# Two transformer blocks on one core: the convolution's sums kept in PSUM, the projections' low parts on GpSimd, layers written out, stage ends made ahead

## What is computed

```python
# first block, per layer
u = modulate(h, ...); y = swiglu_ffn(u, w_gate, w_up, w_down)          # d_ff 2816
h = layer_norm(ALPHA * h + 0.5 * gate * y)
y = hybrid_token_mixer(modulate(h, ...))                               # below
h = layer_norm(ALPHA * h + gate * y)
h = layer_norm(ALPHA * h + 0.5 * gate * swiglu_ffn(modulate(h, ...)))
# hybrid_token_mixer: one projection w_in, then three branches
y_a = silu(layer_norm(causal_dwconv(val * sigmoid(gate), width 31))) @ w_a_out
y_b = mamba2_ssd(...)  (a causal convolution of width 4 first)  @ w_b_out
y_c = nsa_attention(...) @ w_c_out
y = (g0 * y_a + g1 * y_b + g2 * y_c) @ w_o
# second block, per layer
z = rmsnorm(x) @ w_in; att = sliding_window_attention; hm = mlstm_chunkwise
x = x + (gates * (att @ w_att) + gates * (hm @ w_m)) @ w_out
x = x + relu(rmsnorm(x) @ w_ff1) ** 2 @ w_ff2                          # d_ff 4096
```

## Time and profile before

| | us |
|---|---|
| median of 3 runs | 3005.77 (2996.24 to 3027.09) |
| profiled execution, its own time | 3011.23 |
| its span | 3009.4 |
| mean granted TensorE clock in it | 0.944 |

### The profile page before, as it was taken

How to read it: one execution, slowest core, us unless ns; L and a number is a source line. 1 busy time by engine, 2 the same in 40 slices (tenths; PEclk the granted TensorE clock), 3 DMA queues, 4 the chain that set the end, 5 groups by cost and what they waited for, 6 DMA issues and landing times.

```text
span 3009.4 us, 53898 instructions
## 1 busy us (share of the span) xinstructions
PE 2719.9 (90%) x19972; PEld 2530.0 (84%) x19976; DVE 1863.7 (62%) x2968; ACT 1184.6 (39%) x1984; POOL 630.3 (21%) x386
## 2 busy tenths in 40 slices
PE   4998996799989979989788999997978999988999
PEld 4997996678789979979687878996976898876899
DVE  6755987656366675669884653774084575175476
ACT  2444442325334444434332552443442344342344
POOL 2322000000023323310000000332640244540243
PEclk9999997889999999999898999998988999997999
DMA  7757541222367377575322224763431455341453
GB/s 305 279 189 269 201 164 52 100 71 92 120 219 255 135 264 247 189 282 176 119 85 77 99 92 155 262 224 134 139 121 63 148 187 176 120 140 56 140 187 127
DMA packets 131947, 486.18 MB, mean 162 GB/s; under 512 B 15024, under 2 KB 15024, under 8 KB 130352
## 3 DMA queue, kind: packets, MB, share of 16 engines
q1 hardware_dynamic: 106704, 389.09, 37.1%
q0 software_dynamic: 23040, 83.90, 7.6%
q10 hardware_dynamic: 2016, 10.66, 0.9%
HBM read 478.34 MB, written 5.24 MB: 161 GB/s over the span
## 4 chain that ended last, share of the span: by engine, by line
PE 81%; DVE 10%; DVEq 2%; issue 2%; ACT 2%; DMA 2%; ACTq 0%; SPq 0%; POOL 0%; POOLq 0%
PE ps L429 19%; PE ps L431 18%; PE ps L430 18%; PE ps L680 5%; PE ps L2080 2%; PE ps L958 2%; PE ps L2090 2%; DVE ac L1516 2%; PE ps L535 1%; PE ps L440 1%; PE ps L439 1%; PE ps L438 1%; DMA qr<-ada_dram 1%; PE ps L481 1%; PE ps L898 1%
## 5 line engine op out<-in xcount | busy, mean ns | idle before, releaser
L430 PE MATMUL ps<-u_parts,high 128*128 128x256 f32 x3712 | 1060.7, 286 | 0.0
L430 PEld LDWEIGHTS ps<-u_parts,high 128*128 128x128 f32 x3712 | 716.4, 193 | 2.3
L1002 ACT ACTIVATE high<-ring 128x1024 fp32r<-128x1024 f32 x434 | 456.7, 1056 | 456.3 <-PE ps L431 338.4
L429 PE MATMUL ps<-ac_parts,high 128*128 128x256 f32 x1920 | 548.3, 286 | 27.2 <-DVE u_parts L1376 18.2
L429 PE MATMUL ps<-h_parts,high 128*128 128x256 f32 (+1 forms) x1792 | 524.9, 293 | 39.5 <-DVE u_parts L1376 14.8
L431 PE MATMUL ps<-ac_parts,ring_parts 128*128 128x256 f32 x1920 | 546.5, 285 | 0.0
L431 PE MATMUL ps<-h_parts,ring_parts 128*128 128x256 f32 (+1 forms) x1792 | 516.0, 288 | 0.0
L429 PEld LDWEIGHTS ps<-h_parts,high 128*128 128x128 f32 (+1 forms) x1792 | 347.8, 194 | 56.0 <-issue 20.1
L429 PEld LDWEIGHTS ps<-ac_parts,high 128*128 128x128 f32 x1920 | 368.5, 192 | 31.3 <-DVE u_parts L1376 13.3
L431 PEld LDWEIGHTS ps<-ac_parts,ring_parts 128*128 128x128 f32 x1920 | 366.6, 191 | 0.0
L429 PE MATMUL ps<-pt_parts,high 128*128 128x256 f32 x1216 | 345.1, 284 | 11.8 <-DVE pt_parts L1420 11.8
(11 more groups left out here) (391 smaller groups left out, 4500.3 us busy)
## 6 DMA issues: line engine op xcount, KB each, us to landing
ring<-stream_dram SPq DMA_DIRECT2D x736, 512.0 KB, 3.3
xc<-ada_dram POOLq DMA_DIRECT2D x80, 512.0 KB, 6.3
z<-ada_dram POOLq DMA_DIRECT2D x40, 512.0 KB, 8.4
qr<-ada_dram POOLq DMA_DIRECT2D x40, 512.0 KB, 11.2
h_aside<-h ACTq DMA_DIRECT2D x4, 1024.0 KB, 8.1
h<-h_aside ACTq DMA_DIRECT2D x4, 1024.0 KB, 6.3
par<-par_dram ACTq DMA_DIRECT2D x3, 365.0 KB, 6.5
conb<-con_dram ACTq DMA_DIRECT2D x1, 1088.0 KB, 8.7
```

The costliest lines, as they stand in the source:

```text
L429: mm(out, hi, xh, start=start, stop=False, **kw)
L430: mm(out, hi, xl, start=False, stop=False, **kw)
L1002: act(high_of(m, i), chunk_of(m, i), ACT.Copy).then_inc(sem["hi"], 1)
```

## The change

1. Wide and narrow convolution: the running sums are in PSUM banks 0 to 3 instead of SBUF; the last tap writes `ac` or `xc`. Channel tiles go in fours. No low part stands between the taps.
2. Low parts of the 69 chunks ahead of the branches: GpSimd, in order, with 8 loads of each of two modulation groups among them. The 16 gate chunks stay on VectorE.
3. `modulation_rows` after C_GLU pairs 1 and 4 and C_XBC pair 0. The mean of the wide convolution 8 chunks earlier (after C_Q pair 3), the mean of squares before C_VS.
4. Layers written out (Python loops); one continuous ring of slots over layers and blocks.
5. Stage ends: first high parts at the end of the stage before; first low parts among the residual; centred `h` goes to `ac` before the mixer, from where it is stored and read; `whole_h` after the first `hidden_low`; `u` and its low parts interleaved in the second block; parameters and `conb` of the second block loaded early; its first squares straight from the end of the first block; residual and output of the second block by pairs of tiles.
6. Last attention groups: the product with `w_c_out` is begun with six of eight tiles (`three_groups`) before the last values are there.

```diff
 class Stream:
+    def slot(self, l, i):
+        return (self.first(l) + i) % RING
@@ tensor1
         def low_made(i):
-            t.wait_ge(sem["lo_m"], at("lo_m", mix1(i) + 1))
+            if i < C_CK:
+                t.wait_ge(sem["lo_g"], at("lo_g", NF + mix1(i) + 1))
+            else:
+                t.wait_ge(sem["lo_m"], at("lo_m", mix1(i) - FRONT + 1))
...
-        accumulate_ones(0, m.ac, "aconv", 0, con("mean")).then_inc(sem["mu"], 1)
+            if n == 3:
+                t.wait_ge(sem["aconv"], at("aconv", 4))
+                accumulate_ones(0, m.ac, "aconv", 0, con("mean")).then_inc(sem["mu"], 1)
+        rms(1, m.sq_a, 1)
@@ scalar1
-            a.wait_ge(done, done_at(cb + 65))
+            for i in range(cb + 66, cb + 66 + HIGH):
+                later_high(i)
...
-        first_highs(C_MIX)
-        squares(0, m.h, m.u, "cent", 0, 5, park=True)
-        a.wait_ge(sem["aside"], at("aside", 16))
+        squares(0, m.ac, m.u, "cent", 0, 5, park=True)
         high_u(1, m.uhi)
@@ vector1
             low(cb + 3, HIGHS * q + 4)
-            whole_h(2 * q)
             hidden(0, 0)
             hidden_low(0, 0)
             low(cb + 5, HIGHS * q + 6)
+            whole_h(2 * q)
...
-        def conv(dst, src, w, b, taps, lo, hi, signal, between=(), lows=()):
+        def conv(dst, src, w, b, taps, lo, bank_, signal, between=()):
+            sums = lambda n: ps[:, bank_ + (n - lo) // 2, (n - lo) % 2 * S:(n - lo) % 2 * S + S]
             for k in range(taps):
-                for n in range(lo, hi):
+                for n in range(lo, lo + 4):
                     if k == 0:
-                        ts(dst[:, n], src[:, n, 0:S], par(w, n * taps), par(b, n), ALU.mult, ALU.add)
+                        ts(sums(n), src[:, n, 0:S], par(w, n * taps), par(b, n), ALU.mult, ALU.add)
+                    elif k < taps - 1:
+                        stt(sums(n), src[:, n, k:k + S], par(w, n * taps + k), sums(n), ALU.mult, ALU.add)
                     else:
-                        last = stt(dst[:, n], src[:, n, k:k + S], par(w, n * taps + k), dst[:, n], ALU.mult, ALU.add)
+                        stt(dst[:, n], src[:, n, k:k + S], par(w, n * taps + k), sums(n), ALU.mult, ALU.add)\
+                            .then_inc(sem[signal], 1)
-                if k < len(lows):
-                    low_mix(lows[k])
                 v.drain()
-        half = C_GLU + 11 + TAPS_A
-        conv(m.ac, m.apad, "aw", "ab", TAPS_A, 0, 4, "aconv", between=(3, 5, 7, 9), lows=range(C_GLU + 11, half))
-        conv(m.ac, m.apad, "aw", "ab", TAPS_A, 4, ND, "aconv", lows=range(half, C_VS))
+        conv(m.ac, m.apad, "aw", "ab", TAPS_A, 0, 0, "aconv", between=(3, 5, 7, 9))
+        keep_mixed()
+        conv(m.ac, m.apad, "aw", "ab", TAPS_A, 4, 2, "aconv")
@@ gpsimd1
+        for n, i in enumerate(range(C_MIX, C_CK)):
+            low(i)
+            for it, after in ((1, 6), (2, 13)):
+                if after <= n < after + 4:
+                    for k in range(2 * (n - after), 2 * (n - after) + 2):
+                        load_later(ada.group(l, 1, it), k)
@@ every engine, both blocks
-    with v.Fori(0, DEPTH) as l:
+    for l in range(DEPTH):
         layer(l)
@@ scalar2
-        a.wait_ge(sem["layer_done"], at("layer_done", 1))
-        a.dma_start(m.par[:, 0:PAR2["all"]], par_source[bass.ds(l, 1)].rearrange("a p n -> (a p) n"))\
-            .then_inc(sem["par"], 16)
-        a.dma_start(aside, m.h).then_inc(sem["aside"], 16)
@@ vector2
             for n in range(ND):
-                last = stt(m.u[:, n], m.h[:, n], par(gain, n), m.rs, ALU.mult, ALU.mult)
-                last.then_inc(sem["umod"], 1)
+                stt(m.u[:, n], m.h[:, n], par(gain, n), m.rs, ALU.mult, ALU.mult).then_inc(sem["umod"], 1)
+                if n >= 1:
+                    low_u(k, n - 1, uhi)
+            low_u(k, ND - 1, uhi)
```

More of the change, by code:

```diff
@@ L902, in values, with three_groups, last_group @@
             last.then_inc(sem["pv"], 1)
+        def three_groups(n):
+            i = C_PC + n
+            t.wait_ge(landed[stream.slot(l, i)], landed_at(i))
+            for k in range(6):
+                mm(ps[:, 4 + n, 0:S], chunk_tile(m, i, k), m.oT[:, k], start=k == 0, stop=False)
+        def last_group(n):
+            i = C_PC + n
+            for k in range(6, ND):
+                last = mm(ps[:, 4 + n, 0:S], chunk_tile(m, i, k), m.oT[:, k], start=False, stop=k == ND - 1)
+            last.then_inc(done, 1)
         def gate_product(n, bank):
@@ L1382, in whole_h, with residual @@
                     .then_inc(sem["whole"], 1)
-        def residual(k0, i, place, ready):
+        def residual(k0, i, place, ready, lows):
             v.wait_ge(sem["based"], at("based", i + 1))
@@ L1547, in layer @@
             last.then_inc(sem["kpe"], 1)
+        inverse_root(1)
+        for n in range(ND):
+            tt(m.ac[:, n], m.ac[:, n], m.rs, ALU.mult).then_inc(sem["anrs"], 1)
         j = 31
@@ L1920, in pair @@
             return j + 1
-        j = pair(E_Q, j)
+        t.wait_ge(sem["lo_g"], at("lo_g", E_Q + 2))
+        for k in range(ND):
+            t.wait_ge(sem["ulo"], at("ulo", k + 1))
+            for c in range(2):
+                last = product3(mm, ps[:, unit(3 * c), c * S:(c + 1) * S], m, E_Q + c, k, m.uhi2[:, k], m.ulo[:, k],
+                                start=k == 0, stop=k == ND - 1, skip_group_check=True)
+                if k == ND - 1:
+                    last.then_inc(done, 1)
+        j += 1
         j = pair(E_Q + 2, j)
@@ L2115, in down @@
                              m.hidlo[:, f % 3], start=False, stop=last, skip_group_check=True)
+                if last and n in (1, 3, 5):
+                    x.then_inc(pairs, 1)
             x.then_inc(done, 1)
-        up(E_FFN, 0, 0)
+        t.wait_ge(sem["lo"], at("lo", 1))
+        for k in range(ND):
+            t.wait_ge(sem["ulo"], at("ulo", 8 + k + 1))
+            last = product3(mm, ps[:, 4, 0:S], m, E_FFN, k, m.uhi_ffn[:, k], m.ulo[:, k],
+                            start=k == 0, stop=k == ND - 1)
+        last.then_inc(done, 1)
         with t.Fori(0, 3) as it:
@@ L2126, in layer, with scalar2 @@
         down(E_FFN + 63, 31, 31, last=True)
-    with t.Fori(0, DEPTH) as l:
+    for l in range(DEPTH):
         layer(l)
-def scalar2(nc, a, m, sem, stream, par_source, aside):
+def scalar2(nc, a, m, sem, stream, whole):
     ps, con = m.ps, m.con_of
@@ L2328, in layer, with vector2 @@
         hidden_high(31, 31)
-    with a.Fori(0, DEPTH) as l:
+        if l + 1 < DEPTH:
+            for i in range(N2, N2 + HIGH):
+                later_high(i)
+    for l in range(DEPTH):
         layer(l)
-def vector2(nc, v, m, sem, stream):
+def vector2(nc, v, m, sem, stream, pairs, con_b):
     ps, con = m.ps, m.con_of
@@ L2560, in layer @@
         low_down(E_FFN + 63, 64)
-    with g.Fori(0, DEPTH) as l:
+    for l in range(DEPTH):
         layer(l)
```

407 lines of the change are left out of this document (205 added, 202 removed).

## The result

| | before | after |
|---|---|---|
| median | 3008.44 us (2996.24 to 3027.09) | 2867.79 us (2861.56 to 2872.32) |
| profiled execution, its own time | 3011.23 | 2867.85 |
| its span | 3009.4 | 2866.2 |
| mean granted TensorE clock | 0.944 | 0.966 |

The ratio is 0.953, 95% interval 0.947 to 0.958: 4.7% faster. The forecast was 2862 (2835 to 2915); it was 6 us too low.

A forecast was written before the change was run, and what follows sets the result against it. TensorE, busy 90%, bounds the kernel; only its waits and lower-clock time count. Terms sum to 144 us off the profiled 3011.2, so 2867; less 5.5 for lying above the median, 2862 us, 8 in 10 within 2835 to 2915.

The forecast's parts named there:

- cut, mean to keys: Both first-block mixers, TensorE's arrival at the wide convolution's mean to its first keys product: 74.7 us gain.
- mixer's front: Mixer's chunks ahead of the mean: GpSimd's low parts and load issues may stop TensorE, -2 us (bounds +3, -10).
- first FFN to mixer: Stage end: earlier reciprocal, and high part of `u` no longer released by the store; 3.4 us twice, 6.8 gain.
- `whole_h`: FFNs: standing after `hidden_low` it removes 11.8 us of waits, part of which comes back; 9 us gain.
- last attention groups: Work begun early in the last attention groups fills short waits: twice 2.5, 5 us gain.
- half clock elsewhere: Outside the mean-to-keys stretch, less time at TensorE's lower clock after shorter gaps: 5 us gain (0 to 12).
- Convolution: Wide convolution: taps summing in PSUM still cost 0.436 us each, so the mean is ready before TensorE wants it.
- the estimate of 16 us more: Wide convolution: PSUM access overhead on 248 instructions x 65 ns per layer; mean 3 us late, sum 6 us smaller.
- The lead: At the mean: VectorE ready at 413.6, TensorE wanting it at 426.8, so VectorE is 13 us ahead.
- The embedding: VectorE's rotary embedding in the gate chunks, delayed by GpSimd's low parts: 3 us reaching TensorE (0 to 15).
- The blocked case: Rival: GpSimd stops VectorE's convolution taps, TensorE stands 83 us, +96 us per layer, 3054 us; chance of slower 3%.
- Stage ends: FFN, layer and block ends: shorter chains to the first product; with last groups and end, 66.4 us gain.

The follow-up runs named there:

- run 1: The changed kernel with both convolutions' running sums back in SBUF, GpSimd still making all low parts: 3005.8 us, ratio 1.000 to the kernel before.
- run 3: The kernel before with only the wide convolution's sums in PSUM (modulation sums fetched between its halves): 3002.8 us, ratio 1.000.
- run 6: The changed kernel with modulation loads spread one behind each GpSimd low part, and the modulation rows that use them later: 2850.2 us.
- Run 9: The changed kernel with modulation rows later, loads still two by two (third group's one low part later): 2852.5 us, ratio 0.949 to the kernel before.
- run 5: The changed kernel as it is, measured again beside three variants of it on the same chip: 2870.8 us.
- run 2: The kernel before with parts 1 to 3 of the change alone (sums, GpSimd low parts with loads, rows and mean moved): 2940.0 us, ratio 0.978.
- run 7: The changed kernel with `whole_h` back in its old place, before the first `hidden` of each FFN: 2878.0 us.
- run 8: The changed kernel with the centred `h` back in its own place before the mixer and stored from there: 2875.6 us.

## Why the prediction was right

By its own steps, measured between the same instructions of the two traces. The mean is taken at its first record here, so the cut is 101.0 and 90.9 us before, 1.9 longer each than the prediction's, and the front is shorter by as much. (The eight records in the earlier trace rows are only the second half of the mean: it has 16, and the first eight ran before the wait. The prediction's 7.6 us for the statistics holds all the same, since it took eight records at half clock for sixteen at full clock.)

| step | forecast | measured |
|---|---|---|
| cut, mean to keys | 74.7 | 77.8 |
| mixer's front (low parts and loads on GpSimd) | -2 | -12.3 |
| keys' rotation | not seen | 9.5 |
| first FFN to mixer | 6.8 | 6.7 |
| second FFN | 1.8 | 1.7 |
| `whole_h` | 9 | 6.1 |
| layer end, first block | 7.9 | 9.0 |
| block end | 14.4 | 12.4 |
| layer end, second block | 13.4 | 11.8 |
| second block's FFN start | 5.6 | 4.2 |
| last attention groups | 5 | 9.0 |
| end | 2.5 | 5 |
| half clock elsewhere; measured: what is left over | 5 | 2 |
| sum | 144 | 143 |

- **Convolution.** Right in mechanism and size; run 1 shows that the sums' place decides and run 3 that the place is free by itself. The value 0.436 for a tap stands at 0.434. The Trainium skill (Perfetto Trace Analysis, Optimizing Scalar/DVE Operations) gives VectorE a larger access overhead on PSUM, and the estimate of 16 us more from it did not come. The lead was 11.8 instead of 13, with both ends 5 to 6 us later than forecast: TensorE by the front, and VectorE because it waited for the gates' sigmoids in the first half (idle 11.57 us at 312.77), a wait that the forecast did not have. That wait belongs in good part to the front as well: in run 6, with the rows later, the first half's waits from 300 us on fall from 15.5 us to 8.0, and the last tap is done at 410.9 instead of 420.1.
- **The embedding.** The prediction's cut held 3 us for a rotary embedding that GpSimd delays. GpSimd did delay it (four of its instructions took 2.3 to 2.9 us instead of 0.7 in the first layer), but it was done at 501.6 and TensorE reached the keys at 511.1 without a wait, so none of the 3 us arrived. The cut was as long as forecast because its chunks took longer than the prediction's rates give: 24.6 us instead of 22.1 for the eight that now lie in it (0.9 of it waits for low parts), 21.6 instead of 20.5 for the token chunks and 23.2 instead of 22.1 for the gate chunks. One error stood in for another here, which is luck.
- **The blocked case.** The rival's rule was that an instruction with two SBUF inputs waits for GpSimd and one with one does not. The Trainium skill (SBUF — State Buffer, Who interferes with whom) says so, and run 1 beside the changed kernel bears it out (15143 against 493 ns at most). What no row showed, whether a weight column counts as an input, is answered by 493 ns: it doesn't. The step of that rival that failed is its sum, 83 us of standing: it was 55 (110.4 in all), since VectorE gets 1.8 taps per low part and not only the time in which GpSimd is idle. (By its own numbers that time is 130 less 108, so 22 us and not 26.)
- **The front** is the one term that was wrong by more than its bounds (-10). The prediction said that a load "may also land just after TensorE wants it" and priced GpSimd's backlog; the backlog cost 2.5 us in all (PE's waits for low parts by line), and the late landing was nearly all of it. What should have been worked out: the loads behind the 7th to 10th low part are issued until 292.7, they land 7 to 11 us after their issue while the DMA engines move up to 413 GB/s, and the rows come at 295. Run 9 moves the rows by two and four chunks and gets 15 us back against the changed kernel's median and 18 against run 5's. That is more than the term. The two fronts together are 21.3 us shorter than in run 5's profile: 11.4 of it TensorE stood still there, and 9.9 are busy time with the same matmuls, at a mean granted clock of 0.96 and 0.98 instead of 0.93 and 0.95.
- **The keys** waited for VectorE's rotary embedding before, as the release in the earlier trace rows shows: 11.9 and 12.0 us from the keys' first product to the compression's first (L707, now L708), now 7.0 and 7.4. Before, TensorE took them one by one as the embedding finished each, and in part at half clock (0.86 and 0.74 on average); now the embedding is done before they begin. The prediction ended its cut at the keys' first product and so left this out.
- **Stage ends**, last groups and end: nine terms, 66.4 forecast, 65.9 measured, and run 2 leaves 72 to them. `whole_h` gave 6.1 instead of 9, since TensorE now waits for low parts made by VectorE behind it (5.2 us in four waits; 0.3 in run 7); run 7 gives 7.3. For the first entry run 8 gives 4.8 by its median and 7.5 by its trace, where 6.8 had been forecast.
- The errors had both signs (+3.1 cut, -10.3 front, +9.5 keys, -7.0 in the seven terms of entries and ends, +4 last groups, +2.5 end, -3 half clock), which is why the sum came within 1 us of the profiled execution (2867 forecast, 2867.85 measured). That is luck in part: with the front as forecast the kernel would have taken 2858. The 6 us by which the forecast missed the median are no step of it: it took off 5.5 us because the profiled execution before lay that much above its median, and the changed kernel's does not (2867.85 and 2867.79).

**What stays open.** Why the last groups gave 9 and not 5 was not tried. Neither that written-out layers cost nothing nor what the earlier mean is worth was measured alone.

## What to carry to other kernels

Before work goes from VectorE to GpSimd, count the SBUF inputs of what stays on VectorE beside it: here one operand moved to PSUM was worth 138 us, and without it the whole change was worth nothing (run 1). Moved by itself, with nothing on GpSimd beside it, it was worth nothing either (run 3). A load placed behind another engine's work must be timed to its user, by issue plus landing under the traffic of that moment; moving the user back by two to four chunks gave 15 to 18 us. And a wait of TensorE on a serial chain of small VectorE instructions often has an idle stretch of VectorE just ahead of it: look at its timeline there before anything is made faster.

## What the runs showed of the hardware beyond the forecast

- A blocked VectorE instruction can wait for more than one GpSimd instruction. In run 1 the tap that began at 315.09 lasted 15.14 us, through five low parts and the issues of loads between them, which followed each other without a gap; at the same place of the second layer one took 14.6 us. No other tap took more than 2.8 us, and elsewhere a blocked tap did get in between two low parts that had no idle time between them. What makes the difference is open.
- The issues alone do not hold VectorE off. The two taps from 311.60 ran during the two issues from 311.33 and took 0.48 us each (0.88 for both, since their records overlap), and in the kernel before 31 of VectorE's own low parts, with two SBUF inputs, ran beside issues of GpSimd and took 1.22 to 1.23 us, as they did elsewhere (one is shown below, on VectorE's and GpSimd's timelines). Why the tap at 315.09 did not run during the issues from 314.81 is open.

```profile
281.56 1.23 DVE L1492 TENSOR_TENSOR ring_parts<-ring,high 128x1024 fp32r<-128x1024 f32 x1 [4.14 <-ACT high L1002]
...
282.02 1.20 POOL L1798 DMA_DIRECT2D qr<-ada_dram  x2
```

- The exclusion is two-sided: with a tap under way a low part took 2.4 to 2.7 us in run 1 (2.59 in the row shown), alone mostly 2.39.
- TensorE's granted clock also falls without a wait ahead of it. PE's stretches in the kernel before, where the small chunk with its 48- and 16-column products is computed:

```profile
400.00:405.00 5.00, 5.00 (x25) 0.50 0.00 0
405.00:410.00 5.00, 5.00 (x38) 0.86 0.32 108
```

It is busy throughout, and at the lower level, 1.2 GHz, for some 6 us; the changed kernel has the same at 400 to 410 (0.93, 0.73). It wasn't tried whether another place for that chunk avoids it.
